# Column sums of the shift and scale vectors by transposes and a reduction

## What is computed

```
def adaln(c, w_mod, b_mod):
    mod = jax.nn.silu(c) @ w_mod + b_mod
    return jnp.split(mod, 6, axis=-1)
...
def modulate(x, g, shift, scale):
    return rmsnorm_2(x, g) * (1.0 + scale[:, None, :]) + shift[:, None, :]
```

## Time and profile before

| | |
|---|---|
| runs | 2310.56 us (median of 3; 2309.61 to 2310.98) |
| span of the profiled execution | 2310.2 us |
| PE busy | 2265.2 us (98%) |
| DVE busy | 1305.9 us (57%) |
| ACT, POOL busy | 34%, 14% |
| mean granted TensorE clock | 0.998 of full |
| chain of work that ended last | PE 90%, DVE 4%, POOL 2%, rest 1% each or less |

### The profile page before, as it was taken

One profiled execution on the slowest core, in us unless ns is written; L12 is line 12 of the kernel. 1 busy time (PEld: TensorE's weight loads), 2 busy tenths in 40 slices (PEclk: granted clock), 3 DMA queues, 4 the chain that ended last, 5 costly groups with the idle time before them and its releaser, 6 DMA issues.

```text
span 2310.2 us, 30843 instructions
## 1 busy us (share of the span) xinstructions
PE 2265.2 (98%) x11976; PEld 1726.2 (75%) x11976; DVE 1305.9 (57%) x2919; ACT 794.8 (34%) x1707; POOL 326.5 (14%) x349
## 2 busy tenths in 40 slices
PE   7999999999999999999999999999999999999998
PEld 5866576678546667788776888887878678888886
DVE  3565565764246545757767476664368846443334
ACT  4255103531013203723557132223443643222233
POOL 2200110001000012021200100004443001000154
PEclk9999999999999999999999999999999999999999
DMA  7200331002233363022310345553222103322222
GB/s 315 74 20 21 126 110 64 19 19 66 94 119 133 93 218 98 7 76 95 110 38 2 107 163 186 190 184 136 101 92 73 38 1 123 123 100 97 104 94 80
DMA packets 58271, 225.92 MB, mean 98 GB/s; under 512 B 20479, under 2 KB 21119, under 8 KB 41741
## 3 DMA queue, kind: packets, MB, share of 16 engines
q1 hardware_dynamic: 58124, 223.94, 28.4%
HBM read 221.83 MB, written 2.10 MB: 97 GB/s over the span
## 4 chain that ended last, share of the span: by engine, by line
PE 90%; DVE 4%; POOL 2%; ACT 1%; DMA 1%; issue 1%; SPq 1%; POOLq 0%; ACTq 0%; DVEq 0%
PE PS L86 85%; PE PS L91 5%; POOL WKr L103 1%; DMA GB<-in_ev_ada 1%; DVE WK L108 1%; SPq L162 1%; DVE WK L142 1%; ACT WK L98 1%; ACT WKr L96 0%; DVE SM L135 0%; POOL SM L103 0%; DVE WK L115 0%; ACT WK L96 0%; DVE X L115 0%; DVE X L103 0%
## 5 line engine op out<-in xcount | busy, mean ns | idle before, releaser
L86 PE MATMUL PS<-Hr,GBr 128*128 128x512 f32 (+1 forms) x1332 | 440.7, 384 | 0.0
L86 PE MATMUL PS<-Hr,RINGr 128*128 128x512 f32 (+1 forms) x1112 | 409.5, 373 | 0.0
L96 ACT ACTIVATE WK<-PS 128x512 f32<-128x512 f32 (+2 forms) x391 | 189.0, 516 | 450.4 <-PE PS L86 272.1
L86 PE MATMUL PS<-H,RING 128*128 128x512 f32 (+1 forms) x928 | 336.5, 515 | 1.9 <-DVE GB L115 1.9
L115 DVE SCALAR_TENSOR_TENSOR ACC<-ADA,SM,ACC 128x256 f32<-128x256 f32 x608 | 291.3, 502 | 39.5 <-DMA ADA<-in_l_mod 21.4
L86 PEld LDWEIGHTS PS<-Hr,GBr 128*128 128x128 f32 x1332 | 247.6, 188 | 51.1 <-issue 3.9
L86 PEld LDWEIGHTS PS<-H,RING 128*128 128x128 f32 x928 | 172.2, 190 | 138.6 <-issue 128.2
L103 DVE TENSOR_TENSOR RINGr<-RING,GBr 128x1024 fp32r<-128x1024 f32 x148 | 183.6, 1279 | 138.2 <-ACT GBr L96 137.6
L86 PE MATMUL PS<-RING,GB 128*128 128x256 f32 x1152 | 251.2, 379 | 0.0
L86 PEld LDWEIGHTS PS<-RING,GB 128*128 128x128 f32 x1152 | 218.1, 190 | 30.4 <-issue 1.3
L86 PEld LDWEIGHTS PS<-Hr,RINGr 128*128 128x128 f32 x1112 | 208.4, 187 | 37.8
(11 more groups left out here) (222 smaller groups left out, 2823.8 us busy)
## 6 DMA issues: line engine op xcount, KB each, us to landing
ADA<-in_l_mod SPq DMA_DIRECT2D x96, 512.0 KB, 3.7
RING<-in_l_gu SPq DMA_DIRECT2D x44, 1024.0 KB, 4.8
RING<-in_l_wd SPq DMA_DIRECT2D x24, 1024.0 KB, 4.8
RING<-in_ev_in SPq DMA_DIRECT2D x13, 1024.0 KB, 5.8
ADA<-in_od_ada SPq DMA_DIRECT2D x24, 512.0 KB, 3.6
RING<-in_od_in SPq DMA_DIRECT2D x11, 1024.0 KB, 6.0
RING<-in_l_in SPq DMA_DIRECT2D x10, 1024.0 KB, 4.8
RING<-in_l_out SPq DMA_DIRECT2D x8, 1024.0 KB, 4.8
```

What stands on the lines that cost most here:

```text
L86: self.last = self.eng.matmul(out, lhsT, rhs, start=start, stop=stop, skip_group_check=True)
L96: self.last = self.eng.activation(out, in_, func, bias=bias, scale=scale)
```

## The change

For shift and scale PE no longer multiplies each block of `ACC` by a column of ones. It transposes the four blocks by 128 columns of an identity matrix into one bank of 512 columns. DVE sums the 128 columns of each block by one `tensor_reduce` from PSUM to four columns in `SM`, waits for its own result, and adds the bias in place. The scale's second instruction stays. The gate's applies are as they were.

```
-                            pe.matmul(bank(b, f, f + 1), a[:, f * 128:(f + 1) * 128], ones[:, 0:1], True, True)
+                            pe.transpose(bank(b, f * 128, (f + 1) * 128), a[:, f * 128:(f + 1) * 128], ident)
...
-                    ps = bank(where[event], 0, 4)
+                    ps = bank(where[event]).rearrange("p (f c) -> p f c", c=128)
+                    sv = (scalev if kind else shiftv)[st, cd][:, half_ * 4:half_ * 4 + 4]
+                    own(dve.tensor_reduce(sv, ps, AXX, ALU.add).then_inc(dve_value))
                     if kind == 0:
-                        dve.tensor_tensor(shiftv[st, cd][:, half_ * 4:half_ * 4 + 4], ps, bias, ALU.add)
+                        dve.tensor_tensor(sv, sv, bias, ALU.add)
                     else:
-                        sv = scalev[st, cd][:, half_ * 4:half_ * 4 + 4]
-                        own(dve.tensor_tensor(sv, ps, bias, ALU.add).then_inc(dve_value))
+                        own(dve.tensor_tensor(sv, sv, bias, ALU.add).then_inc(dve_value))
                         dve.scalar_tensor_tensor(sv, sv, 1.0, vec(STAGES[st][3], half_ * 4, 4), ALU.add, ALU.mult)
```

## The result

The changed kernel took 2300.37 us (median of 5 runs, 2299.94 to 2301.08), against 2310.22 us (median of 5, 2309.33 to 2310.98) for the kernel before on the same chip: a ratio of 0.9957, with a 95% interval of 0.9945 to 0.9969. The prediction was 2300.0, with 2298.8 to 2303.6 as its range. The same kernel was timed in two more sets of 5 runs, with medians of 2299.89 and 2300.27. Over all 15 runs the median is 2300.27, over the 30 runs of the kernel before in the same three sets 2310.83: a gain of 10.6 us. By the medians of each set it is 9.9, 11.1 and 10.6 us, so the gain is known to about half a us.

A forecast was written before the change was run, and what follows sets the result against it. PE's stream, busy 2265.2 of 2310.2 us, was taken to bound the kernel. PE's 11.0 us less and 0.4 us lost at the tight place gave -10.6 us: span 2299.6, median 2300.0 us, range 2298.8 to 2303.6.

The forecast's parts named there:

- Part 1 and 2: PE at 24 applies: one-column matmuls go (21.5 us), transposes come (10.5 us); 11.0 us less, bounds 10.8 to 11.2.
- rival (c): A transpose of `ACC` is issued as two instructions, nothing gained: 2310.8 us; 4% together with the rule on one-column matmuls.
- The rule on one-column matmuls: Skill's figures make eight one-column instructions (0.20 us) cost no more than four transposes (0.22): 2311.3 us; 4% shared with rival (c).
- Part 3: DVE's part of each apply grows by a 0.68 us reduction and waiting: 0.74 or 0.72 us more, 17.5 us on DVE.
- The tight place: Behind the apply at 640.23 us, DVE's scaled latent rows delay PE's sum of squares: slack 0.97 us, 0.4 us lost.
- Where I could follow, the slack is 3 us or more but for the one place: Behind DVE's applies, PE asks for DVE's results 3 us or more after they are ready, except at the sum of squares.
- no queue of DMAs is moved: POOL clears `ACC` sooner since PE signals sooner, and the change shifts no queue of DMA loads.
- at most 1.2: Rival that DVE's delay reaches PE at more places: at most 1.2 us each; one to six places 6%, slower 2%.
- The bridge from span to median: The runs' median is 0.4 us above the profiled span, and this is kept: span 2299.6, median 2300.0 us.
- Rival (b): Transposes make the granted clock fall, some 1.1 to 1.7 us a place, 2334 us if at all 20 places; chance 2%.

The follow-up runs named there:

- e1: The changed kernel timed and profiled once more, with no further edit: 2299.89 us, ratio 0.9954 to the kernel before.
- e2: PE's half alone: against the kernel before, PE makes the four transposes and DVE reads four columns without the reduction; 2299.77 us, ratio 0.9957.
- e9: The changed kernel once more with no further edit, timed together with e10 and e11: 2300.27 us, ratio 0.9954 to the kernel before.
- e5: Against the changed kernel, each of the 96 transposes is made twice: 2310.34 us, ratio 0.9999 to the kernel before.
- e10: Against the changed kernel, no reductions in the two shift applies of `l0f` ahead of 819 us: 2300.53 us, ratio 0.9956 to the kernel before.
- e7: Against the changed kernel, DVE scales the two latent rows ahead of the apply and accumulations: 2302.41 us, ratio 0.9955 to the kernel before.
- e8: As e7, and SP issues a step's position bias loads behind its load of `RING` weights: 2304.04 us, ratio 0.9968 to the kernel before.
- e11: The kernel of e7 run once more, timed together with e9 and e10: 2300.47 us, ratio 0.9956 to the kernel before.
- e3: DVE's half alone: against the changed kernel, one-column matmuls return on PE and DVE's reduction stays; 2310.69 us, ratio 1.0001 to the kernel before.
- e4: Against the changed kernel, each of the 24 reductions is made twice in a row: 2302.9 us, ratio 0.9966 to the kernel before.

## Why the prediction was right, and where it was not

- **Part 1 and 2, PE: right.** 0.90 and 0.44 us for an apply were the distances read before, and the steps at the places sum to 10.8 us in e1, e2 and e9, where 11.0 was said: 0.15 is missing at two places, with 0.35 and 0.41. The stated bounds of 10.8 to 11.2 hold it, but they do not come out of the distances named for them, which give 10.9 to 11.0. Less the 0.46 at the sum of squares, 10.4 is left in e1 and e9, where 10.6 was said; 9.6 in the first profile of the changed kernel, for the 0.7 lost at 819 us. That the medians of all runs differ by just the 10.6 forecast is in part luck, since the three sets gave 9.9 to 11.1. The 96 instructions in place of 192 speak against rival (c). So does e5, whose twice four transposes are just the case that (c) described: ratio 0.9999.
- **The rule on one-column matmuls: right not to use it, but it was cited in part.** The Trainium skill ("TensorE: Matmul & The Clock Gate", section "Back-to-back issue gap") prices 128 columns at about twice 1 to 64 columns, and gives this table for a single matmul by itself. The same section says that in a stream of weight loads and matmuls "the per-MM spacing is set by *both* ops". With this sentence the page does not speak against the change. The trace does not agree with the table and is in line with the sentence: in e5 eight of the one took 0.88 us and in the earlier trace rows eight of the other 0.90.
- **Part 3, DVE: right in price.** The reduction was put at 0.68 us and took 0.684. The accumulations start 0.79 and 1.01 us after the start of DVE's part, where 0.81 and 1.01 were said. DVE is busy for 1320.8 us, where I said about 1323; the groups that changed grew by 16.6 us of busy time, and the rest of the difference lies in others.
- **The tight place: right, even in size.** 0.4 us was taken, 0.46 is measured, in each of the four profiles with the change's apply and order (after, e1, e9, e10). It is gone in e2 and in the three profiles with the rows first (e7, e8, e11), absent in e3, and 0.72 larger in e4. One reading was wrong without harm: the 0.60 us for the first square is in the earlier trace rows the length of another instruction, and a square took 0.63.
- **"Where I could follow, the slack is 3 us or more but for the one place": wrong.** At the third apply of `l0f`, at 826 us in the profile of before, the accumulations ended at 823.34 and PE asked at 825.60: 2.26 us. I had looked at DVE's queue behind each apply and put it that "no queue of DMAs is moved", and not at a chain over several applies in which SP waits for DVE and DVE for SP's loads. Between 775 and 835 us of the profile after, SP waits 33.6 us in total for DVE's accumulations. In one of three profiles of the changed kernel 0.7 us was lost there. How much of it is the change's stays open (e10). It lay inside the range, as one more place at "at most 1.2".
- **The bridge from span to median: the number held, the reason did not.** I said that the median lies 0.4 us above the span. In each run listed since, the time is 1.8 us above its own span. So the profiled execution of before (2310.2) belongs, worked out from this, to a time of about 2312.0, 1.4 above the median of 2310.56. It had the stretch at half clock at 126 us; whether the runs behind the median had it is not known. The predicted difference of 10.6 was applied to both span and median, and so the error dropped out for the median. For the span it did not: 2299.6 was said, and 2299.1, 2298.1 and 2298.3 came.
- **Rival (b), the clock: wrong here.** The granted clock of the profile after is 1.00 from 28.8 to 2291.9 us, with all of the new transposes. Below full clock there is the one stretch at 25 or 126 us or none, ahead of all edits, and one at the program's end, as in the profile of before.

## What to carry to other kernels

Price PE's instructions by their distance from start to start, and not by their columns: here, with new weights of 128 by 128 for each, one column cost as much as 128 (0.11 us), and a float32 matmul of one column, as two instructions, twice a transpose. When work moves from PE to another engine, the slack behind it shrinks by the sum of what the other engine loses and what PE gains. Follow it also through queues of loads that wait for that engine, since there an edit elsewhere and the scatter of landings come on top.

## What the runs showed of the hardware

A short stretch at half clock (3.4 us, granted clock 0.50) lay at 126 us in three of the profiles (before, e3, e7), at about 25 us in most of the others, and nowhere ahead of the end in e1, e8 and e9. All of these run the same instructions up to 289 us. The profiles that do not have it at 126 us are 1.0 to 2.3 us ahead of the profile of before at 250 us (first column of the tables), those that have it stand at -0.09 and 0.07. In each profile without it at 126 us, 1.6 us of the lead over before come between 124 and 132 us, which is what the stretch costs there; the rest is scatter ahead of it. At 25 us a wait for loads hides it. This alone makes a difference of two single profiles unsafe below 2 us.

Two multiplications of 768 columns on DVE, which mostly take 1.15 us, took some 3.1 us once in the attention stage in the profile after (one of the two took 2.58):

```profile
909.37 3.11 DVE L108 TENSOR_SCALAR WK<-WK,SM 128x768 f32<-128x768 f32 x2
...
912.53 1.09 PE L91 MATMUL PS<-CN,WK 128*128 128x128 f32 x8 [1.12 <-DVE WK L108]
```

PE waits for it. Before, e1, e4 to e8 and e10 have a pair of 3.1 us at about this place too; in e2, e3, e9 and e11 the longest there is 1.7 to 2.5 us. This goes with the scatter of up to 1 us between 850 and 1000 us in the tables, where these four gain 0.8, 1.0, 0.6 and 0.3. e7, which loses 1.0 there, has two such pairs (3.11 and 3.48 us).

The traces show with what the long durations coincide. POOL adds to the position bias at that time, as its loads land, and its row in the profile after is:

```profile
909.69 2.36 POOL L103 TENSOR_TENSOR H<-H,CN 128x960 f32<-128x960 f32 x1 [0.79 <-DMA H<-in_rpb]
```

It ends at 912.05, and the long multiplication, begun at 909.90, at 912.48. In e9 POOL's row comes 1.96 us later, at 911.65, and the pair at 908.96 takes 1.15 us:

```profile
911.65 2.24 POOL L103 TENSOR_TENSOR H<-H,CN 128x960 f32<-128x960 f32 x1 [2.98 <-DMA H<-in_rpb]
```

Each of the 13 profiles has 64 multiplications of this shape and 608 accumulations into `ACC`. Those that take long (multiplications over 0.8 us, accumulations over 0.6) are 11 to 14 in a profile. Each of these overlaps a two-input instruction of POOL (TENSOR_TENSOR) and ends at a fixed distance behind its end, 0.28 us for an accumulation and 0.42 for a multiplication, within 0.01. Without an overlap none took more than 0.63 us. Not every overlap delays: those that ended 1.1 us or more ahead of POOL's instruction kept their usual time. This looks as if DVE were held until POOL is done, and with which instruction it collides here follows the landing of the bias loads. No run moved POOL's work on purpose, so the hold is read from traces and its cause is not tested.
